# Seven block products for the Silu inputs of a two-layer hybrid decoder trunk, weight sums issued earlier, and another split of the opening's work

## The reference, cut to what matters

```python
xn = rms_norm(h, norm_g)                       # h: tokens x 2048
proj = xn @ w_in                               # 2048 -> 15360 columns
a_in, a_b, a_c, a_z, b_in, b_z, c_val, c_gate, c_z, gates = split(proj)   # nine of 1024, gates 3 x 2048
y_a = a_b * conv3(a_c * a_in) * silu(a_z)
y_b = groupwise_linear(trailing_mean_w(b_in) - b_in) * scale * silu(b_z)
v   = dwconv31(c_val * sigmoid(c_gate)) + bias
y_c = silu(layer_norm(v)) * silu(c_z)
merged = sum_b sigmoid(gates[b]) * (y_b @ w_branch_out[b])
h = h + merged @ w_o
h = h + sigmoid(h @ w_pg) * (p[i] @ w_pp)
# twice (DEPTH = 2), then a final rms_norm
```

## Time and profile before

| | |
|---|---|
| Median of 3 runs | 2592.05 us (2591.72 to 2593.22) |
| The profiled execution | 2592.57 us |
| Its span on the slowest core (core 1) | 2591.0 us |
| Spans of the 8 cores | 2585.6 to 2591.0 us, granted clock 0.992 to 0.993 |
| TensorE busy | 2512.6 us (97%), 15468 matmuls |
| VectorE busy | 1560.5 us (60%) |
| ScalarE busy | 556.6 us (21%) |
| GpSimd busy | 119.4 us (5%) |
| Chain of work that ended last | TensorE 89%, VectorE 7%, ScalarE 1% |

### The profile page before, as it was taken

The page is one execution under the profiler, slowest core; times in us unless marked ns, Lnnn a source line. Parts: engine busy times, 40 slices in busy tenths (PEclk is TensorE's granted clock), DMA queues, the critical chain, the costliest instruction groups (busy, mean ns, idle before and its releaser), DMA issues.

```text
span 2591.0 us, 35103 instructions; the slowest of 8 cores (2585.6 to 2591.0 us)
## 1 busy us (share of the span) xinstructions
PE 2512.6 (97%) x15468; PEld 1506.6 (58%) x15468; DVE 1560.5 (60%) x1534; ACT 556.6 (21%) x746; POOL 119.4 (5%) x217
## 2 busy tenths in 40 slices
PE   5999999999999999999999999999999999999997
PEld 2666667776667678766666655544554444444445
DVE  4567666865787753412447676777668885442156
ACT  6000002211212322112340000022112224221124
POOL 0000000000000000000000000000000000000001
PEclk9999999999999999999999999999999999999998
DMA  7434343444344444645553434334434444446453
GB/s 219 88 66 79 69 76 72 82 75 73 73 74 83 92 85 82 143 99 95 132 131 74 75 72 82 73 74 81 86 70 81 91 90 98 83 96 148 84 94 131
DMA packets 49848, 237.51 MB, mean 92 GB/s; under 512 B 4768, under 2 KB 18080, under 8 KB 26912
## 3 DMA queue, kind: packets, MB, share of 16 engines
q0 software_dynamic: 29056, 186.72, 40.1%
q1 hardware_dynamic: 20640, 48.54, 5.6%
HBM read 404.67 MB, written 17.29 MB: 163 GB/s over the span
## 4 chain that ended last, share of the span: by engine, by line
PE 89%; DVE 7%; ACT 1%; SPq 1%; issue 1%; DMA 1%; POOL 0%; DVEq 0%; ACTq 0%; POOLq 0%
PE psa L134 89%; DVE Tt L134 3%; DVE h L134 3%; SPq L134 1%; ACT Tt L134 1%; DVE yb L134 1%; DMA yb<-w_in 1%; DVE acc L134 0%; ACT L134 0%; POOL ring L134 0%; ACT psa L134 0%; ACT yb L134 0%; ACT acc L134 0%; DVEq L131 0%; DVEq L99 0%
## 5 line engine op out<-in xcount | busy, mean ns | idle before, releaser
L134 PE MATMUL psa<-xn,ring 128*128 128x352 bf16 (+8 forms) x8384 | 1365.4, 322 | 9.2 <-DVE Tt L134 5.3
L134 PEld LDWEIGHTS psa<-xn,ring 128*128 128x128 bf16 x8384 | 815.5, 97 | 541.6 <-DVE Tt L134 9.5
L134 DVE SCALAR_TENSOR_TENSOR h<-h,par_s 128x1056 f32<-128x1056 bf16 (+1 forms) x480 | 623.6, 1299 | 11.5
L134 DVE TENSOR_TENSOR Tt<-psa,Tt 128x1056 f32<-128x1056 f32 (+7 forms) x208 | 205.5, 989 | 517.1 <-PE psa L134 477.2
L134 ACT ACTIVATE Tt<-psa 128x512 f32<-128x512 f32 (+9 forms) x328 | 243.2, 742 | 1134.6 <-PE psa L134 1108.2
L134 PE MATMUL psa<-yb,ring 128*128 128x352 bf16 (+1 forms) x1920 | 343.5, 339 | 0.0
L134 PE MATMUL psa<-acc,ring 128*128 128x352 bf16 (+2 forms) x1664 | 292.7, 336 | 31.1 <-DVE acc L134 23.6
L134 PEld LDWEIGHTS psa<-yb,ring 128*128 128x128 bf16 x1920 | 186.5, 97 | 152.2
L134 PEld LDWEIGHTS psa<-acc,ring 128*128 128x128 bf16 x1664 | 161.9, 98 | 159.9 <-DVE acc L134 26.1
L134 DVE TENSOR_TENSOR Tt<-Tt 128x1056 f32<-128x1056 f32 (+9 forms) x130 | 136.0, 1046 | 121.3 <-ACT Tt L134 118.3
L134 PE MATMUL psa<-h 128*128 128x264 bf16 (+1 forms) x1152 | 185.1, 319 | 17.6 <-DVE h L134 16.0
(11 more groups left out here) (70 smaller groups left out, 928.9 us busy)
## 6 DMA issues: line engine op xcount, KB each, us to landing
ring<-w_in POOLq DMA_DIRECT2D x118, 1024.0 KB, 9.0
ring<-w_branch_out POOLq DMA_DIRECT2D x24, 1024.0 KB, 9.0
ring<-w_o POOLq DMA_DIRECT2D x16, 1024.0 KB, 9.6
ring<-w_ple_gate POOLq DMA_DIRECT2D x14, 1024.0 KB, 11.0
h<-xT SPq DMA_DIRECT2D x12, 724.0 KB, 15.7
h<-xT SPq DMA_DIRECT2D x16, 543.0 KB, 8.9
h_keep<-h SPq DMA_DIRECT2D x16, 543.0 KB, 8.8
h<-h_keep SPq DMA_DIRECT2D x16, 543.0 KB, 8.5
```

The source lines that it names most:

```text
L134: ins = getattr(eng, o.meth)(**o.kw)
```

## The change

The Silu inputs of branches A and B (both layers) and of branch C (layer 1 only) are made by `block_group` instead of two `mm_group` calls: 8 slots in layer 0, 12 in layer 1. `block_group` takes the function, an own place for the half result p4 (`m5`) and for `u` as arguments; both lie in the `yb` tiles that the unit writes later. `weight_sums` of a slot is recorded one step ahead of its use, also for the first gate slot of each merge. The numbers of taps per place change. In C the two projections of a unit now stand ahead of its two normalisations. In the opening, every fourth scaled copy is ScalarE's instead of every second, fewer `xn` tiles are made between the pieces, and GpSimd converts both halves of the late slot.

```diff
-                    if k % 2:
+                    if k % 4 == 3:
                         ACT(xg, src, AF.Copy, reads, [r_xgt[t][k]], scale=norm_col(l, k))
...
-                        xn_part(0, range(4 * i4, 4 * i4 + 4))
+                        xn_part(0, range(2 * i4, 2 * i4 + 2))
...
+            stage_cast(1, 0, "pool")
+            stage_cast(1, 1, "pool")
             for i4 in range(4):
                 piece(2, i4, 4, 6)
-                xn_part(1, range(4 * i4, 4 * i4 + 4))
-            stage_cast(1, 0, "act")
-            stage_cast(1, 1, "pool")
+                xn_part(0, range(8 + 2 * i4, 10 + 2 * i4))
...
-                xn_part(2, range(5 * t, 5 * t + 5 + t // 2))
+                if t < 2:
+                    xn_part(1, range(8 * t, 8 * t + 8))
+                else:
+                    xn_part(2, range(16))
...
+            def yscratch(k):
+                return yb[:, k, :].bitcast(F32), [r_yb[k]]
+
-            def block_group(slot, rows, base, pend):
+            def block_group(slot, rows, base, pend, func=AF.Sigmoid, m5=None, u3=None):
...
-            def merge_branch(b):
+            def merge_branch(b, slot):
                 pend = deque()
-                slot = load_gate(0)
-                weight_sums(slot)
...
                     bo = load_main512(w_bo[l, b, q])
-                    block_group(slot, (2, 3), 0 if nb == 2 else 4, pend)
-                    bg(4)
+                    block_group(slot, (TF(2), TF(3)), 0 if nb == 2 else 4, pend, u3=TF(5))
+                    bg(5)
...
-                        bg(1)
+                        if jj == 0:
+                            bg(2)
+            zbase = 0 if nb == 2 else 4
```

Branch A, the end of a unit, then branch B:

```diff
                 for i in range(2):
                     g = mm_group(proj_steps(slot, i * 128, xn, r_xn), R_out)
                     TT(v3(co, R_out), pv(g, R_out), v3(co, R_out), ALU.mult, g.res + r_co, r_co)
+                    if i == 0:
+                        weight_sums(z_slot)
+                    bg(2)
+                if j == 3:
+                    slot = load_gate(0, 0)
+                pend = deque()
+                block_group(z_slot, tA, zbase, pend, AF.Silu, yscratch(u[0]), yscratch(u[1]))
+                if j == 3:
+                    weight_sums(slot)
+                while pend:
+                    pend.popleft()()
+                for i in range(2):
+                    TT(yb[:, u[i], LO:TL], cv[i][0][:, LO:TL], tA[i][0][:, LO:TL], ALU.mult, ...)
                     bg(3)
...
+                    if i == 0:
+                        weight_sums(z_slot)
+                if j == 3:
+                    slot = load_gate(1, 0)
+                pend = deque()
+                block_group(z_slot, Z, zbase, pend, AF.Silu, yscratch(u[0]), yscratch(u[1]))
+                if j == 3:
+                    weight_sums(slot)
+                while pend:
+                    pend.popleft()()
+                bg(6)
+                state["pg"] = 0
                 ss = load_side(pool_w[l, j])
                 for o in range(2):
                     g = mm_group(steps, R_out)
                     STT(v3(yb[:, u[o], :], R_out), pv(g, R_out), ...)
+                state["pg"] = 0
```

Branch C:

```diff
+            def cz_block(j, nxt):
+                pend = deque()
+                if l == 0:
...
+                    return
+                block_group(cz_slot[j], (TF(0), TF(1)), zbase, pend, AF.Silu, yscratch(2 * j), yscratch(2 * j + 1))
+                if nxt is not None:
+                    weight_sums(nxt)
+                while pend:
+                    pend.popleft()()
...
+            cz_slot = [load_main(wl[(8 * E) // 256], 16)]
+            if l > 0:
+                weight_sums(cz_slot[0])
             bg(len(bgq))
+            cz_slot.append(load_main(wl[(8 * E + 256) // 256], 16))
+            cz_block(0, cz_slot[1])
...
             for j in range(1, 4):
+                cz_slot.append(load_main(...) if j < 3 else load_gate(2, 0))
+                cz_block(j, cz_slot[j + 1])
                 for i in range(2):
-                    cz_norm(*cz_proj(j, i))
+                    cz_norm(2 * j + i, *TF(i))
```

More of the change, by code:

```diff
@@ L632, in block_group @@
                 p4, q4 = bank(b4)
-                ua, r_u = TF(4 + rows[0] // 2)
-                u3 = ua[:, 0:H].rearrange("p (j n) -> p j n", n=N)
+                ua, r_u = u3
+                u3 = tiled(ua[:, 0:H])
                 g00, r00 = half(rows[0], 0)
@@ L638, in block_group @@
                 g11, r11 = half(rows[1], 1)
+                if m5 is None:
+                    m5v, r_m = g11, r11
+                else:
+                    m5v, r_m = tiled(m5[0][:, 0:H]), m5[1]
                 prod(b0, wq(0, 0), xh(0, 0), True)
@@ L757, in build_program @@
                     TT(v3(co, R_out), pv(g, R_out), v3(co, R_out), ALU.mult, g.res + r_co, r_co)
-                    bg(3)
-                slot = load_main(wl[(3 * E + u[0] * 128) // 256], 16)
-                for i in range(2):
-                    g = mm_group(proj_steps(slot, i * 128, xn, r_xn), R_out)
-                    sz, r_sz = tA[i]
-                    co, r_co = cv[i]
-                    ACT(v3(sz, R_out), pv(g, R_out), AF.Silu, g.res, r_sz)
-                    TT(yb[:, u[i], LO:TL], co[:, LO:TL], sz[:, LO:TL], ALU.mult, r_co + r_sz, [r_yb[u[i]]])
-                    bg(3)
-            merge_branch(0)
+                    if i == 0:
[10 more added lines that the diff above has]
+                for i in range(2):
+                    TT(yb[:, u[i], LO:TL], cv[i][0][:, LO:TL], tA[i][0][:, LO:TL], ALU.mult, cv[i][1] + tA[i][1], [r_yb[u[i]]])
+                    bg(3)
+                state["pg"] = 0
+            merge_branch(0, slot)
             for j in range(4):
@@ L776, in build_program @@
                 slot = load_main(wl[(4 * E + u[0] * 128) // 256], 16)
+                z_slot = load_main(wl[(5 * E + u[0] * 128) // 256], 16)
+                Z = [TF(5), (pTs[:, :, :].rearrange("p a t -> p (a t)").bitcast(F32), [r_p])]
                 for i in range(2):
@@ L797, in build_program @@
                     TT(Pi[:, HALO:HALO + 16], tmp16[:, :], Ui[:, HALO:HALO + 16], ALU.subtract, [r_tmp16] + r_Ui, r_Pi)
-                slot = load_main(wl[(5 * E + u[0] * 128) // 256], 16)
-                for i in range(2):
-                    g = mm_group(proj_steps(slot, i * 128, xn, r_xn), R_out)
-                    ACT(v3(U[i][0], R_out), pv(g, R_out), AF.Silu, g.res, U[i][1])
-                    bg(3)
+                    if i == 0:
[9 more added lines that the diff above has]
+                bg(6)
+                state["pg"] = 0
                 ss = load_side(pool_w[l, j])
@@ L806, in build_program @@
                     g = mm_group(steps, R_out)
-                    STT(v3(yb[:, u[o], :], R_out), pv(g, R_out), pcol(PB + 24 + u[o]), v3(U[o][0], R_out), ALU.mult, ALU.mult,
-                        g.res + [r_par] + U[o][1], [r_yb[u[o]]])
-            merge_branch(1)
-            def cz_proj(jj, i):
-                g = mm_group(proj_steps(cz_slot[jj], i * 128, xn, r_xn), R_out)
-                Z, r_Z = TF(i)
-                ACT(v3(Z, R_out), pv(g, R_out), AF.Silu, g.res, r_Z)
-                return 2 * jj + i, Z, r_Z
+                    STT(v3(yb[:, u[o], :], R_out), pv(g, R_out), pcol(PB + 24 + u[o]), v3(Z[o][0], R_out), ALU.mult, ALU.mult,
+                        g.res + [r_par] + Z[o][1], [r_yb[u[o]]])
+                state["pg"] = 0
+            merge_branch(1, slot)
+            def cz_block(j, nxt):
+                pend = deque()
+                if l == 0:
+                    for i in range(2):
+                        g = mm_group(proj_steps(cz_slot[j], i * 128, xn, r_xn), R_out)
+                        Z, r_Z = TF(i)
+                        ACT(v3(Z, R_out), pv(g, R_out), AF.Silu, g.res, r_Z)
+                    if j == 3:
+                        weight_sums(nxt)
+                    return
+                block_group(cz_slot[j], (TF(0), TF(1)), zbase, pend, AF.Silu, yscratch(2 * j), yscratch(2 * j + 1))
+                if nxt is not None:
+                    weight_sums(nxt)
+                while pend:
+                    pend.popleft()()
             def cz_norm(ui, Z, r_Z):
```

43 lines of the change are left out of this document (23 added, 20 removed).

## The result

The changed kernel takes 2719.2 us (median of 4 executions, three of them at 2718.2 to 2719.6) against 2592.5 (4 executions, 2591.7 to 2593.2) in the same comparison: a ratio of 1.0487, interval 1.0467 to 1.0508. That is slower by 126.7 us. The forecast was 2700 with a range of 2666 to 2724: right side, inside the range, and short by 19.

The account below looks back on a forecast made before the run. TensorE, busy 97%, was taken to bound the kernel, so saved columns pay unless waits open. Terms -14.3 - 13.4 + 4.7 + 62.1 + 13.1 + 2.0 + 18.4 + 34.9 = +107.5 on 2592.6 gave 2700 us, range 2666 to 2724.

Parts of the forecast that it names:

- dear restarts: Throughout: matmuls restarting slowly after each wait, priced at 2.5 us each, would give 2708 us.
- rival 1: Layer 1's C: clock stays at 1.2 GHz through five products, each run costing 8.65 us; 2727 us, chance 0.10.
- The three large terms: Branch B +62 us, the entries to C +34, and C's units in layer 1 +35.
- Opening: Start of the kernel: late gate matmuls start as before; 0, bounds ±2 us.
- A's columns: Branch A, both layers: all 8 units keep their saved matmul columns; -14.3 us.
- Merge 0's starts: Start of merge 0, both layers: waits of 5.00 and 5.14 us and slow matmuls behind them go; -13.4 us together.
- B in layer 0: To merge 1's second group: taps behind the additions free the pooling banks late; +29.1 us.
- B in layer 1: To merge 1's second group: taps behind the additions free the pooling banks late; +33.0 us.
- Entries to C: Before C: 19 taps in a row instead of four hold TensorE; +13.1 us in layer 0, +18.4 in layer 1.
- C's units in layer 1: ScalarE's copy, queued behind two normalisations' Silus, delays each block group's third product; +34.9 us to merge 2's second group.
- The restart, 1.9 us: Slow clock after each TensorE wait: 1.9 us, taken eight times in B and four around layer 1's C.
- Rivals 2 and 3: Layer 1's C copies not late, 2656 us, chance 0.05; B's banks freed in time, savings whole, about 2543, chance 0.05.

Follow-up runs that it names:

- opening_old: Changed kernel with only the opening put back to that of the kernel before: 2720.0 us.
- a_yb_first: Changed kernel with both yb products ahead of the six taps in branch A's last unit: 2713.5 us, one execution.
- b_taps_last: Changed kernel with branch B's six taps recorded behind the two results of the pooling matrix instead of ahead of them: 2653.3 us.
- b_bank: Changed kernel with the two b_in groups of layer 1's branch B in banks 3 to 5 and 0 to 2, instead of the reverse: 2712.4 us, one execution.
- a_more_taps: Changed kernel with six taps instead of two behind the second half of a_b in branch A, leaving 3 instead of 19 before C: 2685.2 us.
- c_pair: Changed kernel with each unit's two normalisations interleaved in layer 1's branch C, block order kept: 2710.2 us.
- c_pend: c_pair with each interleaved pair moved behind the three copies of the next block group, the last inside merge 2's first group: 2679.4 us.
- c_ahead: Changed kernel with the next unit's block group recorded ahead of the current unit's two normalisations in layer 1's branch C: 2720.7 us.
- best1: Changed kernel with b_taps_last, a_more_taps, a_yb_first, b_bank; C (merge 2's weight sums moved), merge taps and opening as before: 2550.9 us, again 2552.7.
- best2: Same as best1, except that C keeps the changed kernel's form, with c_pend in layer 1: 2560.0 us.
- c_plain: Changed kernel with layer 1's branch C making its Silu inputs by the ordinary projection again, the 19 taps kept: 2682.4 us.

## Why the prediction was right, and where its sizes were off

**The number: partly luck.** The prediction allowed 2708 for dear restarts and some 8 us for miscounts, which is 2716. The measured 2719 lies above that, in the part of the range that was added towards rival 1, and rival 1 didn't happen. What filled it were waits that the prediction had not seen and slow products that it had priced too low, nearly all on one side. The three large terms were right in place, kind and nearly in size. Its reading of the waits before was also too short: h was not the largest kind; acc was, with 23.6 us in seven, but 16.1 of them are the first wait of the execution and the sum doesn't use them.

**Opening: right in kind.** It was given 0 with bounds of 2; by the rows of V's start it lost 0.6, and by opening_old its worth is below what two runs tell apart.

**A's columns: right.** The stretch to merge 0 got 6.6 shorter in layer 0, which is the 7.2 less the 0.6 above.

**Merge 0's starts: the term failed by half.** The forecast took the removal of the 5 us waits at full price, -13.4. The waits on h are gone, but each start got a new one of 2.4 and 2.6 us, on ScalarE's first copy. The step that failed was to take what lies behind a removed wait as coming whole: I named as late next only VectorE's entry into the merge, and didn't follow the second Silu tile, which is freed by the second yb, behind three taps (397.40 above). a_yb_first showed this cause. Measured: -6 in all, 7.8 missing (3.9 a layer).

**B in layer 0: right to 0.1 us as a sum** (+29.0 for 29.1). Units at 591.55, 629.65 and 667.49 are 38.1 and 37.8 apart, where 38.5 was expected; the last unit took 41.9 for 41.0, and merge 1's first group with its restart 15.1 for 14.5. That these cancel to 0.1 is luck; each is within 1 us. b_taps_last showed the mechanism and its size for both layers.

**B in layer 1: 5.6 short.** The waits on yb were there, as forecast. What was missed is a wait of 1.1 to 1.2 us in front of each block group (1886.98 above): its first bank is still being read by ScalarE's copy of b_in's second group. The four waits are 4.6 us together. b_bank removed them and took 6.9 off this stretch, so this term alone is enough for the gap.

**Entries to C: right in mechanism, low by 2.9 and 1.7.** 19 taps ran 25.05 us for 25.2 forecast, and TensorE waited 10.73 and 13.34 for them. In layer 0 the statistics behind the wait then took 5.95 us for what had taken 3.3 (21 matmuls, 913.86): a restart of 2.6 that I had priced at nothing in layer 0. In layer 1 they took 5.04 (14 matmuls, at 2222.82) for 3.23, so the 0.5 given there was 1.3 short. a_more_taps showed the cause.

**C's units in layer 1: right** (+35.5 for +34.9), four waits of 11.26, 8.01, 8.01 and 7.57, units of 22.5, 23.2 and 21.8 for 22.5. c_pair and c_pend showed that the queue of ScalarE and the length of the chain ahead of the copy set them. c_ahead showed that my first cure for it was wrong.

**The restart, 1.9 us, was a little low.** The first product after a wait takes 3.38 us from start to start (2242.57 to 2245.95) and the second 2.27, where 1.73 is usual: 2.2 us lost; the other three of C lost 1.6 to 2.9, and B's 1.4 to 2.9. The granted clock was 0.50 until 2245.9, 0.75 on the way to 2248.2 and 1.00 after it. A sum with 2.5 for each was inside the range, 2708.

**Rival 1, the clock that stays down, is refuted.** By the third product after the wait at the latest, matmuls run at the upper level in every unit of C: 1.73 us from start to start from 2248.22 on, at a granted clock of 1.00. The Trainium skill's page "TensorE: Matmul & The Clock Gate", section "HAM oscillation — how this bites in real kernels", describes a wait per tile that sends the clock down each time. The rows agree with that much, since every one of these waits was followed by slow matmuls; but the clock came back within two products, so the price was a fifth to a third of the 8.65 that the rival gave. Rivals 2 and 3 fell with the four late copies and the yb waits.

**What the missing 19.6 us are:** merge 0's starts 7.8, B of layer 1 5.6, entries to C 4.6, and 1.6 spread over the rest.

**What stays open.** Against the changed kernel the single cures give 66 + 34 + 37 + 6 + 7 = 150, which would be 2570; best1 is at 2553. Of these 17 us, 6 are C of layer 0, seen in best2; the merges' taps as before are worth some 4 by the table (+2.6 and +1.7). The last 7 have their place in the rows: c_plain, the single cure for C, still waits 4.32 at merge 2 of layer 1 and loses 2.4 in slow products behind it, 6.7 together, and best1 has no such wait. That the cures don't overlap otherwise is a sum and not a test. Nor did a run combine best1 with the normalisations inside the next group and the first copy ahead of rstd's two steps.

## What to carry to other kernels

When a group of matmuls is made cheaper by copies between its products, each such copy becomes an instruction for which TensorE waits in the middle of the group: look at what is queued ahead of it on its engine, and when that work can start, before counting a column saved. Fill-in work belongs behind the instruction that frees a bank and never in front of it; here that one line was worth 66 us, and with the fill-in work placed right, block products in A and B are 1.6% faster than the kernel before, where the change as a whole was 4.9% slower. When a phase is relieved of background work, the work comes due somewhere, and a queue that is emptied in one piece before a phase shows up as one long wait.

## What the runs showed of the hardware that was not expected

Two conversions on GpSimd took 4.62 us together, starting at 54.78, where one takes 1.89. VectorE ran updates of xn with two inputs in SBUF until 55.70, so the first conversion overlapped them for 0.92 us; the excess is 0.84. The Trainium skill, page "SBUF — State Buffer", section "🔬 SBUF: two separate sides", says that a GpSimd operation that reads SBUF and a VectorE operation with two SBUF inputs exclude each other on a shared pair of ports. The trace agrees. The first of the two conversions took 2.66, and the second, with VectorE done, 1.89; in opening_old, with VectorE idle beside it, it was 1.89 as well. On the other seven cores of the same execution VectorE's updates were not done when the conversions came, and there VectorE paid: the same eight updates took 7.39 to 7.42 us instead of 4.13 (on core 0 two of them 2.22 us each instead of 0.59), and the two conversions 4.03 to 4.48.

The price of a wait for TensorE was 1.4 to 2.9 us above the wait itself, after the waits of 6.5 to 11.3 us in B and C. Over the whole kernel it can be read from busy times: the changed kernel's TensorE was busy for 2512.3 us and best1's for 2476.3, though best1 has 4 x 1.78 = 7.1 us more of columns. So slow matmuls took some 43 us (36.0 and 7.1), a third of the whole loss.

The length of a wait alone doesn't settle whether slow matmuls follow. In c_pend the wait of 3.72 us at 2232.96 was followed by 8 matmuls in 3.59 us, at a granted clock of 0.50; in best2 the wait of 3.72 at 2114.91 was followed by 8 in 1.90, at 1.00. In the 30 us or so before them TensorE had waited 13.33, 1.77 and 1.62 us in c_pend, and 1.52 and 1.49 in best2. No run was made to show what decides.
